# Turning x and B of the state-space mixer on VectorE and through DRAM instead of on TensorE, in token blocks two to four

## The chip, the cores and the metric

The kernel runs on one core of a Trainium2 chip. The metric is device time in microseconds (us), the median over executions; the kernel before has 2672.59 us (three runs, 2672.24 to 2672.9). Engines: TensorE (PE, its weight loads are PEld), VectorE (DVE), ScalarE (ACT), GpSimd (POOL); SyncE (SP) issues nearly all DMAs.

## The reference, cut to what matters

One hybrid decoder layer on 2048 tokens plus 16 meta tokens, float32, model width 1024. The mixer has a pooling part and a state-space part (SSD) with 4 groups of 6 heads of 64 channels, state size 128, chunks of 128 tokens. Then come an output projection, a feed-forward layer of 4096 and a norm.

```python
hn = rms_norm(h, norm_mix_w)
u, z, xbc, dt_raw = split(hn @ w_in)           # 512 | 1536 | 1536+512+512 | 24
xbc = silu(causal_dwconv(xbc))                 # x, B, C
# per group and chunk of 128 tokens; a_cs = cumsum(dt * a)
y_diag = ((C B^T) * decay) @ (x * dt)          # decay = exp(a_cs[l] - a_cs[s]), causal
state  = B^T @ (x * dt * decay_to_end)         # carried: S = S * chunk_decay + state
y_off  = (C @ S) * exp(a_cs)
y = (y_diag + y_off + d_skip * x) * silu(z)    # then a norm over the group's 384 channels
h = h + concat(pool(u), y) @ w_out
h = h + relu(rms_norm(h) @ w1)**2 @ w2
```

The convolution wants channels on the partitions and tokens along the row; `y_diag` and `state` want x and B with tokens on the partitions. Between the two stands a transpose of x (384 channels a group) and B (128 channels), and that is what is changed.

## The kernel before, in words

**Blocks and units.** The tokens go through the mixer in four blocks of 512 (`b` = 0 to 3; the prose counts them one to four), each with four chunks of 128 (`c`). The input projection is cut into units of 128 output columns. A group `g` has eight: unit 0 is B, 1 is C, 2 to 4 are x, 5 to 7 are z. Every product is split into high and low parts and made of three matmuls (`up_unit`). In blocks two to four the z units are computed as four pieces, one a chunk (`z_unit`), so a group there has nine items: five convolution units and four z pieces.

**From a unit to its tile.** TensorE fills one of two PSUM banks; ACT empties it (`evac`: four instructions for a convolution unit, which first wait until the item two before is finished); VectorE applies three taps (`taps`, L2387); ACT takes a tanh; VectorE finishes the SiLU (`finish`: L2417 for a convolution unit, L2403 for a z piece) into a tile of `F` (`group_tile`). The tiles of groups g and g+1 alternate.

**Steps.** A step `q` is one chunk of one group, 16 a block. `mixer_plan` lays step (g-1, c) beside items 2c and 2c+1 of group g (c = 3 also takes item 8); steps 12 to 15 have pool units beside them. TensorE's order in a step: unit `n1`; transposes of y of step q-2 (L2011); `diagonal` of q-1 (L2023); `slot1`: four transposes of x and B (L1985) into bank 4 or 5, then C B^T (L1991); `state` of q-1 (L2040); the unit or units `n2`; `y_offset` (L2003). In steps 12 to 15 there is no `n1`. `state` waits for `yo_ready`, the instruction L2600 of VectorE, which has emptied bank 7.

**VectorE's order in a step:** `y_finish` of q-1 (L2463, L2465), `state_add` (L2473), the taps of `n1`, the mask (L2555), the decay product (L2572), the low part of B (L2577), x times dt (L2583) and x times its weight (L2587), the low parts of y and of that product (L2486, L2478), `finish` of the item before and of `n1`, then L2600, then the taps of `n2`. `Steps.link` makes an instruction wait for the one before it on its own engine.

**ACT's order:** `evac` of n1, a tanh, the high part of C (L1526), six instructions of the decay (L1533), the exponential (L1539), the copies of B and x out of PSUM (L1547, L1549), then squares, the norm of y (L1433), high parts (L1428), the evacuation of n2.

**SyncE's queue** issues in program order: the weights of unit n when unit n-4 is done (`load`, L788, two DMAs of 512 KB a unit, a ring of four), the running sums (L804), the next block's x, h. Nothing is computed ahead by a planner; the order is written out as above. Everything outside the blocks' mixer (output projection, feed-forward) is not touched by the change. Block one (`b` = 0) uses plain, unsplit matmuls for `y_offset` and `state` and has z transposes besides.

Of the kernel before, what the change touches and what calls it, by code (L numbers as in the profile page):

```python
# [167 lines left out]
def build(nc, x, meta, norm_mix_w, w_in, pool_w, pool_scale, conv_w, conv_b, dt_bias, a_log,  # L168
          d_skip, ssm_norm_w, w_out, norm_ffn_w, w_ff1, w_ff2, norm_f_w, out):
    ctx = ExitStack()  # L170
    with ctx:
# [37 lines left out]
        xb = sb("xb", [P, GW])  # L209
        xdt = sb("xdt", [P, GW])  # L210
        xw = sb("xw", [P, GW])
        zs = sb("zs", [P, GW])
# [12 lines left out]
        acsT = win_tmp[0:HEADS, 0:TB]  # L225
        sums = sb("sums", [P, CH, HEADS_PER_GROUP, P])
# [30 lines left out]
        b_plain = at("b_plain", [P, 2, P], h_at + 9216)  # L257
# [31 lines left out]
        hn_scr = nc.dram_tensor("hn_scr", [3, 2, P, 4, TB], F32).ap()  # L289
        sums_scr = nc.dram_tensor("sums_scr", [BLOCKS, GROUPS, CH, HEADS_PER_GROUP * P], F32).ap()  # L290
# [15 lines left out]
        def per_head(t, c, g, rows=P):  # L306

            o = c * HEADS + g * HEADS_PER_GROUP
            return t[0:rows, o:o + HEADS_PER_GROUP].unsqueeze(2).to_broadcast(
                [rows, HEADS_PER_GROUP, HEAD])  # L310

# [44 lines left out]
        xb_ps = sig("xb_ps", STEPS)  # L356
        zc_ps = sig("zc_ps", STEPS)
        z_late = sem("z_late")
        xb_ready = sig("xb_ready", STEPS)
# [40 lines left out]
        w2_loaded = [sem(f"w2_loaded{i}") for i in range(5)]  # L400
# [15 lines left out]
        p_ps, p_hi, p_lo = sem("p_ps"), sem("p_hi"), sem("p_lo")  # L416
# [31 lines left out]
        def dt_bank(b):  # L448
            return bank[2] if b else bank[3]

# [179 lines left out]

        def w2_source(q):
# [70 lines left out]
        with nc.Block() as block:  # L702

            @block.sync
            def _(sp):
# [44 lines left out]
                initial = [s for s in signals if s.start and s not in (state_ready, *sums_loaded)]  # L750
# [56 lines left out]

                def load_quarter(i):
# [14 lines left out]
                for b in range(BLOCKS):  # L823
                    N0 = b * UNITS
                    for n in range(RING, U_OUT):
                        load(N0 + n, in_unit(n))
                        if b == 0 and RING < n < RING + 3:
                            meta_pair(POOL_PAIR + n - RING - 1)
                        if n == (8 if b else 12):
# [16 lines left out]
                    for d in range(2):  # L846
                        for i, kp in enumerate(OUT_ORDER):
                            load(N0 + U_OUT + d * 8 + i,
                                 w_out[0, kp * 256:(kp + 1) * 256, d * 512:(d + 1) * 512
                                       ].rearrange("(k p) c -> p k c", p=P))  # L850
                            if b < LAST and (d, i) == (0, 3):
# [3 lines left out]
                            if (d, i) == (0, 4 if b else 6):  # L855
                                yoff_ps.wait(sp, b, STEPS)
                                state_ps.wait(sp, b, STEPS)
                                sp.dma_start(h[:, :, :], x_in[0, b * TB:(b + 1) * TB, :].rearrange(
# [184 lines left out]
            def _(pool):  # L1043
# [61 lines left out]
                for b in range(BLOCKS):  # L1105
# [4 lines left out]
                    for q, g, c, n1, n2 in mixer_plan(b):  # L1110
# [12 lines left out]
                        xb_ready.wait(pool, b, q + 1)  # L1123
                        gated.wait(pool, b, q)
                        steps.link(nc.gpsimd.tensor_tensor(by_head(ty[:, :]), by_head(xb[:, :]),
# [105 lines left out]
                def second_sum(c, name):  # L1231
# [7 lines left out]
                    for x in {"t1": ("11", "12"), "t2": ("22",), "t3": (), "t4": ("21",)}[name]:  # L1239
                        l = 4 * c + W2_QUARTERS.index(x)  # L1240
                        pool.wait_ge(w2_loaded[l % 5], 16 * (l // 5 + 1))
# [31 lines left out]
            def _(act):  # L1273
# [42 lines left out]

                def evac(b, v):
# [3 lines left out]
                    up_out.wait(act, b, v - 1)  # L1321
                    piece = piece_of(b, v)
# [1485 lines left out]
```

## Time and profile before

| | |
|---|---|
| median of the runs | 2672.59 us |
| profiled execution, first to last instruction (span) | 2674.7 us |
| TensorE busy | 2654.5 us, 99% of the span |
| VectorE / ACT / GpSimd busy | 1636.3 / 1281.4 / 1091.7 us |
| TensorE's granted clock, mean | 0.999 |
| DMA traffic | 531.14 MB, mean 199 GB/s |

The profile comes from one execution; of that one the page has the span, which stands 2.1 us above the median of the unprofiled runs. Busy time says how much an engine does, not whether it is waited for; for that one reads the idle time of TensorE and what ended it, and then the timeline of a step, engine by engine. In a timeline row the third column is the engine, "x3" a number of instructions merged, and brackets give the idle time before the row and what ended it.

### The profile page before, as it was taken

What the parts mean: (1) busy time and instruction counts of PE and PEld (TensorE: products, weight loads), DVE (VectorE), ACT (ScalarE), POOL (GpSimd) and SP (SyncE); (2) the same over time, 40 slices, a digit from 0 to 9 for tenths busy, and PEclk for the clock granted to TensorE, in tenths of its full rate; (3) what the DMA queues carried; (4) which work ended last, traced back from release to release, by engine and by line L of the source; (5) the groups of instructions that cost most, each with busy time, mean ns of one, the idle gap of its engine ahead of it and who ended that gap; (6) DMA issues with size and microseconds to landing.
All of it is one profiled execution on the core that took longest, in us unless ns stands there. A gap on an engine that the chain in (4) does not pass through costs nothing.

```text
span 2674.7 us, 37670 instructions
## 1 busy us (share of the span) xinstructions
PE 2654.5 (99%) x14058; PEld 2225.0 (83%) x14058; DVE 1636.3 (61%) x2204; ACT 1281.4 (48%) x2562; POOL 1091.7 (41%) x866
## 2 busy tenths in 40 slices
PE   8999999999999999999999999999999999999998
PEld 6788778888888888898888888888888888888887
DVE  6788714788136883367853576574445766666667
ACT  4577654666245672355734454555454322222223
POOL 2133440335003441023444688665554535353434
PEclk9999999999999999999999999999999999999999
DMA  9977676654646546555574555774445842423324
GB/s 327 299 255 244 237 247 223 251 181 172 220 174 245 194 160 236 190 215 181 188 267 142 200 197 203 259 259 154 152 151 207 309 145 96 164 103 126 118 95 157
DMA packets 224451, 531.14 MB, mean 199 GB/s; under 512 B 14074, under 2 KB 97022, under 8 KB 214798
## 3 DMA queue, kind: packets, MB, share of 16 engines
q1 hardware_dynamic: 224270, 528.74, 55.3%
q8 instruction: 112, 1.84, 0.3%
q14 instruction: 69, 0.57, 0.1%
HBM read 382.74 MB, written 145.95 MB: 198 GB/s over the span
## 4 chain that ended last, share of the span: by engine, by line
PE 95%; DMA 2%; SPq 1%; DVE 1%; issue 0%; POOL 0%; ACT 0%; POOLq 0%; ACTq 0%
PE bank L2257 23%; PE bank L2225 22%; PE bank L1832 21%; PE bank L1939 12%; PE bank L1919 7%; PE bank L2023 2%; PE bank L1985 1%; PE bank L2040 1%; PE bank L2003 1%; PE bank L2011 1%; DMA w_scr<-w_both 1%; DMA meta_w<-in_w_in 1%; PE bank L1991 1%; PE bank L1958 1%; DMA raw<-in_w_out 0%
## 5 line engine op out<-in xcount | busy, mean ns | idle before, releaser
L1832 PE MATMUL bank<-hnT_hi,w_ring 128*128 128x512 f32 x1152 | 369.4, 392 | 0.0
L2257 PE MATMUL bank<-w_first,T_hi 128*128 128x512 f32 x896 | 275.8, 389 | 0.0
L2387 DVE SCALAR_TENSOR_TENSOR acc<-pre,par,acc 128x512 f32<-128x512 f32 x240 | 211.6, 882 | 90.4 <-ACT pre L1345 84.6
L1832 PEld LDWEIGHTS bank<-hnT_hi,w_ring 128*128 128x128 f32 x1152 | 216.3, 188 | 44.5 <-ACT win_tmp L1474 0.5
L2742 DVE TENSOR_TENSOR acc_th<-bank,acc_th 128x512 f32<-128x512 f32 x224 | 150.0, 686 | 155.4 <-PE bank L2257 154.0
L2225 PE MATMUL bank<-T_hi,w_both 128*128 128x512 f32 x768 | 242.4, 389 | 0.5 <-DVE ff L2683 0.5
L1939 PE MATMUL bank<-w_ring,T_hi 128*128 128x512 f32 x768 | 239.0, 392 | 0.1
L1832 PE MATMUL bank<-hnT_lo,w_ring 128*128 128x512 f32 x576 | 224.5, 390 | 0.0
L2257 PEld LDWEIGHTS bank<-w_first,T_hi 128*128 128x128 f32 x896 | 168.2, 188 | 34.9
L1919 PE MATMUL bank<-w_ring,hnT_hi 128*128 128x384 f32 x768 | 196.0, 336 | 0.0
L1832 PE MATMUL bank<-hnT_hi,w_both 128*128 128x512 f32 x544 | 183.1, 408 | 2.3 <-ACT pre L1345 2.3
L2225 PE MATMUL bank<-b,w_both 128*128 128x512 f32 x768 | 179.5, 389 | 0.0
L2257 PE MATMUL bank<-T_hi 128*128 128x512 f32 x448 | 174.3, 389 | 0.0
L2257 PE MATMUL bank<-T_lo,T_hi 128*128 128x512 f32 x448 | 174.3, 389 | 0.0
L2257 PE MATMUL bank<-w_first,T_lo 128*128 128x512 f32 x448 | 174.3, 389 | 0.0
L2257 PE MATMUL bank<-T_hi,T_lo 128*128 128x512 f32 x448 | 174.3, 389 | 0.0
L2225 PEld LDWEIGHTS bank<-T_hi,w_both 128*128 128x128 f32 x768 | 144.1, 188 | 31.2 <-DVE ff L2683 1.3
L2225 PEld LDWEIGHTS bank<-b,w_both 128*128 128x128 f32 x768 | 144.0, 188 | 30.3 <-DVE ff L2675 0.5
L1939 PEld LDWEIGHTS bank<-w_ring,T_hi 128*128 128x128 f32 x768 | 142.5, 188 | 30.0 <-DVE y L2465 1.3
L1630 ACT ACTIVATE w_both<-w_sum 128x512 fp32r<-128x512 f32 x128 | 81.0, 633 | 172.5 <-PE bank L2225 138.9
L2225 PE MATMUL bank<-hnT_hi,w_both 128*128 128x512 f32 x512 | 163.1, 389 | 0.0
L1706 ACT ACTIVATE T_hi<-third 128x1024 fp32r<-128x1024 f32 x56 | 56.3, 1053 | 220.4 <-PE bank L2257 207.7
(315 smaller groups left out, 6315.2 us busy)
## 6 DMA issues: line engine op xcount, KB each, us to landing
w_ring<-w_scr SPq DMA_DIRECT2D x312, 512.0 KB, 4.3
T_scr<-stage SPq DMA_DIRECT2D x32, 1792.0 KB, 6.7
w_scr<-w_both SPq DMA_DIRECT2D x100, 512.0 KB, 4.3
pair_raw<-in_w_ff SPq DMA_DIRECT2D x36, 1024.0 KB, 5.6
third<-T_scr SPq DMA_DIRECT2D x28, 1024.0 KB, 4.9
pair_raw<-T_scr SPq DMA_DIRECT2D x28, 1024.0 KB, 4.9
sums<-sums_scr SPq DMA_DIRECT2D x64, 384.0 KB, 5.0
raw<-in_w_in SPq DMA_DIRECT2D x36, 512.0 KB, 6.4
```

The costliest lines, as they stand in the source:

```text
L1630: nc.scalar.activation(hi, left_source(g), ACT.Copy).then_inc(w1_hi, 1)
L1706: nc.scalar.activation(hi[:, k, :], t_raw[x % 2][:, k, :], ACT.Copy).then_inc(t_hi, 1)
L1832: mm = nc.tensor.matmul(bank[s][:, :], w[:, k, :], t[:, k, :], start=(k == 0 and j == 0), stop=(k == KT - 1 and j == 2))
L1919: mm = nc.tensor.matmul(bank[s][:, 0:GW].rearrange("p (u c) -> p u c", c=P), t[:, k, tok], w[:, k, :, :], start=(k == 0 and j == 0), stop= ...
L1939: mm = nc.tensor.matmul(bank[4 + t][:, :], a, w[:, kk, :], start=(u == 0 and kk == 0 and j == 0), stop=(u == 7 and kk == 1 and j == 2))
L1958: mm = nc.tensor.transpose(dst[:, t * P:(t + 1) * P], h[:, t, k * P:(k + 1) * P], ident[:, :])
L1985: mm = nc.tensor.transpose(bank[4 + q % 2][:, i * P:(i + 1) * P], group_tile(g, j)[:, cols], ident[:, :])
L2023: mm = nc.tensor.matmul(bank[6][rows, r * HEAD:(r + 1) * HEAD], E[:, r, rows], xdt[:, r * HEAD:(r + 1) * HEAD], start=True, stop=True, til ...
L2225: mm = nc.tensor.matmul(bank1(p, m), w[:, k, :], t[:, k, :], start=(m not in (2, 7, 3) and k == 0 and j == 0), stop=(m not in (1, 6, 5) an ...
L2257: mm = nc.tensor.matmul(bank[4 * half + t][:, :], a[:, k, tok], w[:, k, :], start=(SECOND[q % 7] not in GOES_ON and k == 0 and j == 0), st ...
L2387: ins = nc.vector.scalar_tensor_tensor(acc[:, s, 0:TB], pre[:, s, k:k + TB], w, acc[:, s, 0:TB], ALU.mult, ALU.add)
L2742: ins = nc.vector.tensor_tensor(dst, src, dst, ALU.add)
```

## The change

In block one, TensorE still transposes; ACT copies x and B in one instruction into a new tile `xt` with a place for each of the four chunks. In blocks two to four:

- VectorE's `finish` of B and of the three x units writes the SiLU in place (B into its tile, since C B^T still needs it there), then, behind a link, turns it with `nc.vector.transpose`. That turns each 32x32 block in itself and leaves the blocks where they were.
- ACT's queue stores the turned tile, 256 KB, to a DRAM scratch, behind the evacuation of the item two later.
- SyncE's queue loads a chunk with four DMAs, each to 32 partitions, 16 pieces of 32 floats (128 bytes) a partition, so that the blocks come to their places. It waits until the group's four tiles are stored and the same chunk of the group before is used up.
- The four transposes of a step go from TensorE, and ACT's copy of x out of PSUM; the copy of B stays, from `xt`. VectorE and GpSimd wait for the chunk's DMAs in place of `xb_ready`.
- Semaphores are shared anew, `zs` moves, and block one's load of h waits for the last gated y.

```diff
                 def load_tokens(b, g, c):
+                    xt_stored.wait(sp, b, 48 * (g + 1))
+                    b_stored.wait(sp, b, 16 * (g + 1))
+                    ... # waits for xw_ready, ty_ready of the chunk's last user
+                    blocks = xt_scr[b, g, :, :, c * P:(c + 1) * P].rearrange(
+                        "t (i a) (j f) -> j a (t i) f", a=32, f=32)
+                    for j in range(4):
+                        sp.dma_start(xt[32 * j:32 * j + 32, c, :].rearrange("p (k f) -> p k f", f=32),
+                                     blocks[j]).then_inc(xt_loaded[c].sem, 16)
...
+                        if b and g and j in (0, 3, 4, 5):
+                            load_tokens(b, g - 1, (0, 3, 4, 5).index(j))
...
+                            if b and d == 0 and i < 2:
+                                load_tokens(b, GROUPS - 1, 2 + i)
...
                 def evac(b, v):
...
+                    evacuate(b, v, s, ps)
+                    store_turned(b, v - 2)
...
-                        xb_ps.wait(act, b, q + 1)
-                        ty_ready.wait(act, b, q)
-                        xw_ready.wait(act, b, q)
...
-                        nc.scalar.activation(xb[:, :], bank[4 + q % 2][:, 0:GW], ACT.Copy
-                                             ).then_inc(xb_ready.sem, 1)
+                        if b:
+                            xt_loaded[c].wait(act, b, 64 * (g + 1))
+                            state_ps.wait(act, b, q - 1 if q else 0)
+                            nc.scalar.activation(b_both[q % 2][:, 0, :], xt[:, c, GW:GW + P],
+                                                 ACT.Copy).then_inc(b_hi_ready.sem, 1)
...
-                    xb_ready.wait(pe, b, q - 1 if q else 0)
-                    for i, j in enumerate((2, 3, 4, 0)):
-                        mm = nc.tensor.transpose(bank[4 + q % 2][:, i * P:(i + 1) * P],
-                                                 group_tile(g, j)[:, cols], ident[:, :])
-                    mm.then_inc(xb_ps.sem, 1)
+                    if b == 0:
+                        ... # the same five lines
...
+                        dst = group_tile(g, 0) if j == 0 else pre[:, s, 0:TB]
+                        steps.link(nc.vector.scalar_tensor_tensor(dst, pre[:, s, 0:TB], 1.0,
+                                                                  acc[:, s, 0:TB], ALU.add,
+                                                                  ALU.mult))
+                        if j == 0 and g:
+                            b_stored.wait(dve, b, 16 * g)
+                            sums_stored.wait(dve, b, 16 * GROUPS)
+                        nc.vector.transpose(turn_tile(g, j), dst).then_inc(up_out.sem, 1)
```

VectorE in the third step (c = 2) of a group in block three, before, from the decay product to L2600:

```order
L2572 TENSOR_TENSOR E<-E,bank 128x768
L2577 TENSOR_TENSOR b_both_60<-bank,b_both_60 128x128
L2583 TENSOR_TENSOR xdt<-xb,dtt 128x384
L2587 TENSOR_TENSOR xw<-xb,dte 128x384
L2486 TENSOR_TENSOR T_lo<-bank,T_hi 128x3x128
L2478 TENSOR_TENSOR xw_both<-xw,xw_both 128x384
L2417 SCALAR_TENSOR_TENSOR F<-pre,acc 128x512 x2
L2600 TENSOR_TENSOR yo<-bank,ea 128x384
```

And the same place with the change (its line numbers are those of the changed kernel):

```order
L2650 TENSOR_TENSOR E<-E,bank 128x768
L2656 TENSOR_TENSOR b_both_59<-xt,b_both_59 128x128
L2662 TENSOR_TENSOR xdt<-xt,dtt 128x384
L2666 TENSOR_TENSOR xw<-xt,dte 128x384
L2564 TENSOR_TENSOR T_lo<-bank,T_hi 128x3x128
L2556 TENSOR_TENSOR xw_both<-xw,xw_both 128x384
L2489 SCALAR_TENSOR_TENSOR pre<-pre,acc 128x512
L2495 STREAM_TRANSPOSE F<-pre 128x512
L2489 SCALAR_TENSOR_TENSOR pre<-pre,acc 128x512
L2495 STREAM_TRANSPOSE F<-pre 128x512
L2679 TENSOR_TENSOR yo<-bank,ea 128x384
```

Two items are finished in this step, both of x: two more instructions stand ahead of the one that empties bank 7. In the steps c = 0 and c = 1 one such instruction is added, in c = 3 none.

TensorE at the same place of a step, before:

```order
L2003 MATMUL bank<-s_both,c_both 128x384 x3
L2011 MATMUL bank<-ident,y 128x128 x3
L2023 MATMUL bank<-xdt,E 64x64 x12
L1985 MATMUL bank<-ident,F 128x128 x4
L1991 MATMUL bank<-F 128x128
L2040 MATMUL bank<-xw_both,b_both_60 128x384 x3
```

With the change:

```order
L2068 MATMUL bank<-s_both,c_both 128x384 x3
L2076 MATMUL bank<-ident,y 128x128 x3
L2088 MATMUL bank<-xdt,E 64x64 x12
L2056 MATMUL bank<-F 128x128
L2106 MATMUL bank<-xw_both,b_both_59 128x384 x3
```

The four transposes are gone; C B^T and `state` follow `diagonal` at once.

SyncE's queue in block three, from the weights of the first three pool units to the next block's x, before:

```order
L788 DMA w_ring<-w_scr 128x1024 x6
L804 DMA sums<-sums_scr 128x768
L788 DMA w_ring<-w_scr 128x1024 x8
L853 DMA F<-in_x 128x4x1024
```

With the change:

```order
L809 DMA w_ring<-w_scr 128x1024 x6
L842 DMA xt<-xt_scr 32x16x32 x4
L825 DMA sums<-sums_scr 128x768
L809 DMA w_ring<-w_scr 128x1024 x2
L842 DMA xt<-xt_scr 32x16x32 x4
L809 DMA w_ring<-w_scr 128x1024 x2
L842 DMA xt<-xt_scr 32x16x32 x4
L809 DMA w_ring<-w_scr 128x1024 x4
L895 DMA F<-in_x 128x4x1024
```

Chunks two, three and four of the last group each stand behind weights that came before them in the queue.

## Rows read from the trace of the kernel before

**Rows 1.** The page's busy times, and TensorE's granted clock in 40 slices.

```profile
PE 2654.5 (99%) x14058; PEld 2225.0 (83%) x14058; DVE 1636.3 (61%) x2204; ACT 1281.4 (48%) x2562; POOL 1091.7 (41%) x866
...
PEclk9999999999999999999999999999999999999999
```

**Rows 2.** TensorE's waits: who, for whom, us in total, times, longest.

```profile
PE bank L1811 <- DVE F L2280: 5.8, 1, 5.8
```

**Rows 3.** Costliest groups by form, TensorE: the transposes of x and B, all blocks.

```profile
L1985 PE MATMUL bank<-ident,F 128*128 128x128 f32 x256 | 41.7, 286 | 0.0
```

**Rows 4.** Timeline of TensorE at slot1 of a third step: start, us, engine.

```profile
951.28 0.66 PE L1985 MATMUL bank<-ident,F 128*128 128x128 f32 x4
951.77 0.39 PE L1991 MATMUL bank<-F 128*128 128x128 f32 x2
```

**Rows 5.** Busy time from diagonal to L2600, block three, one group.

```profile
923.40:962.40 39.00, 39.00 (x257) 34.33 (x258) 36.72 (x54) 26.63 (x73) 15.23 (x20) 1.00 0.55 200
```

**Rows 6.** Timeline of that stretch: VectorE's links and the end at state.

```profile
923.38 0.56 DVE L2463 TENSOR_TENSOR y<-bank,ty 128x384 f32<-128x384 f32 x1 [5.65 <-PE bank L2023]
937.39 0.56 DVE L2463 TENSOR_TENSOR y<-bank,ty 128x384 f32<-128x384 f32 x1 [0.66 <-PE bank L2023]
938.72 0.56 DVE L2473 TENSOR_TENSOR S<-bank,S 128x384 f32<-128x384 f32 x1 [0.19 <-PE bank L2040]
...
948.81 2.79 DVE L2387 SCALAR_TENSOR_TENSOR acc<-pre,par,acc 128x512 f32<-128x512 f32 x3 [0.43 <-ACT pre L1345]
960.70 1.28 DVE L2417 SCALAR_TENSOR_TENSOR F<-pre,acc 128x512 f32<-128x512 f32 x2
961.90 0.55 DVE L2600 TENSOR_TENSOR yo<-bank,ea 128x384 f32<-128x384 f32 x1
...
963.29 0.60 PE L2040 MATMUL bank<-xw_both,b_both 128*128 128x384 f32 x2
```

**Rows 7.** Timeline of VectorE ahead of the steps: three linked taps.

```profile
776.87 2.33 DVE L2387 SCALAR_TENSOR_TENSOR acc<-pre,par,acc 128x512 f32<-128x512 f32 x3 [3.41 <-ACT pre L1345]
```

**Rows 8.** Groups by form of VectorE in the stretch of rows 5 and 6.

```profile
L2387 DVE SCALAR_TENSOR_TENSOR acc<-pre,par,acc 128x512 f32<-128x512 f32 x15 | 14.4, 962 | 0.8 <-ACT pre L1345 0.4
L2417 DVE SCALAR_TENSOR_TENSOR F<-pre,acc 128x512 f32<-128x512 f32 x5 | 3.3, 685 | 0.0
L2577 DVE TENSOR_TENSOR b_both<-bank,b_both 128x128 fp32r<-128x128 f32 x3 | 0.9, 284 | 0.0
```

**Rows 9.** Timeline of steps 2 and 3, the first group of block three.

```profile
840.29 0.56 DVE L2473 TENSOR_TENSOR S<-bank,S 128x384 f32<-128x384 f32 x1 [0.19 <-PE bank L2040]
849.41 0.55 DVE L2600 TENSOR_TENSOR yo<-bank,ea 128x384 f32<-128x384 f32 x1
...
850.85 0.78 PE L2040 MATMUL bank<-xw_both,b_both 128*128 128x384 f32 x3
```

**Rows 10.** Timeline of steps 13 and 14 of block three.

```profile
985.36 0.26 ACT L1547 ACTIVATE b_both<-bank 128x128 fp32r<-128x128 f32 x1
985.51 0.48 ACT L1549 ACTIVATE xb<-bank 128x384 f32<-128x384 f32 x1
988.85 0.61 ACT L1433 ACTIVATE y<-y,small 128x384 f32<-128x384 f32 x1
989.74 0.49 PE L2011 MATMUL bank<-ident,y 128*128 128x128 f32 x3
```

**Rows 11.** Timeline of SyncE's queue behind the last z piece.

```profile
972.43 2.73 SPq L788 DMA_DIRECT2D w_ring<-w_scr  x6
```

**Rows 12.** Busy time and DMA share while those weights move.

```profile
975.00:981.00 6.00, 6.00 (x29) 5.04 (x28) 5.84 (x11) 4.81 (x13) 3.19 (x5) 1.00 1.02 406
```

**Rows 13.** DMA packets while 96-byte pieces move, then 512-byte ones.

```profile
DMA packets 813, 0.12 MB, mean 202 GB/s; under 512 B 759, under 2 KB 813, under 8 KB 813
...
DMA packets 563, 0.29 MB, mean 320 GB/s; under 512 B 7, under 2 KB 562, under 8 KB 563
```

**Rows 14.** DMA issues of the page: x count, KB each, us to landing.

```profile
h_scr<-h SPq DMA_DIRECT2D x16, 512.0 KB, 2.6
```

More of the change, by code:

```diff
@@ L399, in build @@
         split_loaded = [sem(f"split_loaded{i}") for i in range(3)]
-        w2_loaded = [sem(f"w2_loaded{i}") for i in range(5)]
+        w2_loaded = [xt_loaded[i].sem if i < CH else sem("w2_loaded4") for i in range(5)]
         w2_sum_ready, w2_hi, w2_lo = sem("w2_sum_ready"), sem("w2_hi"), sem("w2_lo")
@@ L749, in _ @@
                     meta_pair(j)
-                initial = [s for s in signals if s.start and s not in (state_ready, *sums_loaded)]
+                initial = [s for s in signals if s.start and s not in (state_ready, xb_ps, xb_ready, b_hi_ready,
+                                                             *sums_loaded)]
                 for j in range(4, POOL_PAIR):
@@ L1121, in _ @@
                             inverse_root(b, rsy[:, :], ssy[:, :], ssy_ready, q, rsy_ready, 1)
-                        xb_ready.wait(pool, b, q + 1)
+                        x_tokens(pool, b, q)
                         gated.wait(pool, b, q)
-                        steps.link(nc.gpsimd.tensor_tensor(by_head(ty[:, :]), by_head(xb[:, :]),
+                        steps.link(nc.gpsimd.tensor_tensor(by_head(ty[:, :]), by_head(xt[:, c, 0:GW]),
                                                            per_head(dsk, 0, g), ALU.mult))
@@ L1315, in _, with store_turned @@
                 steps = Steps(act, act_sem)
+                def store_turned(b, v):
+                    n = unit_of(b, v) if b and v >= 0 else None
+                    if n is None or n >= U_POOL or n % UNITS_G not in (0, 2, 3, 4):
+                        return
+                    g, j = divmod(n, UNITS_G)
+                    act.dma_start(xt_scr[b, g, j - 2 if j else 3], turn_tile(g, j)
+                                  ).then_inc(xt_stored.sem if j else b_stored.sem, 16)
                 def evac(b, v):
@@ L1512, in _ @@
                             acsT_ps.wait(act, b, 1)
+                            if b:
+                                b_stored.wait(act, b, 16)
                             nc.scalar.activation(acsT, bank[3][0:HEADS, :], ACT.Copy
@@ L2423, in finish @@
                     up_evac.wait(dve, b, v + 1)
+                    if b:
+                        b_stored.wait(dve, b, 16 * GROUPS)
                     E_ = TB + 16
```

79 lines of the change are left out of this document (59 added, 20 removed).

## The prediction, made before the changed kernel ran

> **What bounds the kernel now.** I read the page's busy times first: TensorE is busy 99% of the span at its upper clock level, 2.4 GHz, the others 61% or less [rows 1]. Then its waits: the longest, 5.8 us, lies ahead of the blocks, and none is in the steps of blocks two to four [rows 2]. So each us taken from TensorE's queue there is a us of the kernel, as long as nobody it waits for becomes late. Then the cost of what goes [rows 3, 4]. Last, because the change loads VectorE, how near VectorE is to being waited for. Over the whole span it has 39% to spare, but an average says nothing here: in the 39 us of the first three steps of a group it is busy 36.72 [rows 5], since five convolution units are finished there, and idle only 5.65 us in the fourth step, just ahead [rows 6]. This is the view on which I decide.
>
> **What goes from TensorE.** Four transposes stand between diagonal and C B^T; from the first of them to C B^T 951.77 - 951.28 = 0.49 us pass [rows 4]. Their group has 41.7 us for 256 [rows 3], but a busy time leaves out overlap, so I take the distance of starts. 192 go: 48 steps by 0.49 = 23.5 us. That is the most the change can give.
>
> **What comes to VectorE.** 48 transposes of 128x512, 16 a block, and a link ahead of each. The trace has no VectorE transpose. Nearest rows: three linked instructions of 512 elements take 2.33, 0.78 each [rows 7]; two finishes without a link take 1.28, with 0.69 for the second, so the distance of two starts is 0.59 [rows 6, 8]. A finish with link and a transpose then take 0.78 + 0.59 = 1.37 in place of 0.59: x = 0.78 us for each turned tile. Bounds: an instruction of 128 elements takes 0.28 [rows 8], its start distance some 0.1 less, and with the link (0.19) x = 0.37, were the transpose so short; with both linked instructions at the taps' mean of 0.96, which GpSimd's work beside them makes long, x = 0.96 + 0.96 - 0.59 = 1.33. I take 0.78: the same operand width on the same engine, beside finishes that no one lengthens (mean 685 ns).
>
> The Trainium skill (VectorE: DVE Perf Modes, Rules for kernel authors) speaks against the change: a 128x128 transpose belongs on TensorE if PSUM will do as its destination, and VectorE is fastest only for 32x32. Its table of the three transpose paths gives 311 ns for a 128-column VectorE transpose. The nearest row has 284 ns at that width [rows 8]; by the page x would be some 0.03 more, an estimate, and the sum below 0.9 us more.
>
> **A group of three steps, where the two meet.** Follow VectorE from 923.38 in block three [rows 6]. It finishes B in c = 0 (+x), but had 0.66 us idle before y at 937.39, waiting for TensorE, and 0.19 before S at 938.72: it takes both up. In c = 1 one tile of x is turned (+x); 0.43 idle at 948.81, waiting for ACT, whose evacuation hangs on the unturned C tile, is taken up too. In c = 2 two tiles of x are turned (+2x), back to back, right ahead of L2600. So L2600 ends later by 4x - (0.66 + 0.19 + 0.43) = 4x - 1.28 = 1.84 us: 964.29 in place of 962.45. TensorE needs that end for state, which began at 963.29, 0.84 later. It would now come to it 4 x 0.49 = 1.96 earlier, at 961.33, and stands idle from there to 964.29. Against before, the stretch is longer by 1.84 - 0.84 = 1.00: the whole 1.96 is lost and 1.00 with it. This holds for the second and third group of units of each of three blocks: 6 x 1.00 = 6.0 us.
>
> In the first group of a block VectorE still waits for TensorE at the start of step 2 [rows 9]; TensorE is up to 1.5 us ahead there, so VectorE comes out of that wait at best 0.19 earlier than before and then has the two turned tiles: 2x - 0.19 = 1.37 later, with 850.85 - 849.96 = 0.89 to spare: 0.48 longer, three times: 1.4 us. Each of the nine stalls ends with a semaphore's way, some 0.05: 0.5 us.
>
> **Steps 12 to 15.** No tile is turned there, so the 0.49 could come through. But TensorE's next link is close: the norm of y ends at 988.85 + 0.61 = 989.46 and the transposes of y start at 989.74 [rows 10]. The norm stands behind ACT's high part of the weighted x, and that behind VectorE, diagonal and the exponential, so it does not move when ACT's copy of x (0.48) goes. I take 0.28 a step, bounds 0 and 0.49: 12 x 0.28 = 3.4 us gained, at most 5.9.
>
> **Edits at nothing.** ACT: 48 copies of x of 0.48 go [rows 10], 48 issues of some 0.45 come (six issues of SyncE take 2.73 [rows 11]); in the dense third step the issue lies ahead of a tanh that waits for VectorE's taps anyway; uncovered it would be 0.45 each in 9 third steps, 4 us. The four turned tiles ahead of a block's first step: VectorE idles 3.41 us ahead of an item's taps there [rows 7]; uncovered 4x a block, 9 us. SyncE: 192 issues; four stand ahead of the sums of the running decay once a block, 1.8 us, with the z pieces as cover; uncovered 5 us in all. Weights of the ring are asked for three units ahead. Block one, its single copy by ACT and the moved waits: TensorE's queue there is unchanged.
>
> **The sum.** 6 x 1.00 + 1.4 + 0.5 - 3.4 = +4.5 us; in general 30x - 18.9. The profiled span of 2674.7 would become 2679.2. The median of the runs lies 2.1 below the span; the same difference put on it gives **2677.1**. x = 0.37 gives -7.8, x = 1.33 gives +21; x = 0.63 is the point where nothing changes.
>
> **The chunk loads, and a rival from them (B).** Only chunk 1 of the last group is near: its four DMAs stand behind six of weights, issued from 972.43 [rows 11], and 3.15 MB at 406 GB/s [rows 12] take 7.7 us; with one us for the first packet to come, an estimate, they end at 981.2. A chunk is 2048 pieces of 128 bytes over 16 engines. Where 96-byte pieces move, 813 packets pass in 0.6 us, 11.8 ns an engine's packet; where 512-byte ones do, 563 in 0.9 us, 25.6 ns [rows 13]. So the chunk takes 1.5 to 3.3 us; I take 1.7, as the size is near the smaller. A store of 512 KB, 1.3 us by the same rate, lands after 2.6 [rows 14], so 1.3 is added: 984.2. ACT wants it at 985.36 [rows 10], or 0.28 earlier. It comes 0.9 us before that: no cost. Rival B: pieces of a row 2 KB apart cost more than those of rows 13, the chunk comes late, and ACT, GpSimd and VectorE stand in step 13 of each block, TensorE behind them. It decides from (0.9 + 1.7) / 128 = 20 ns a piece; at 25.6 it adds 0.7 us a block, 2 in all, at 60 it adds 5.1, 15 in all: 2679 to 2692.
>
> The Trainium skill (DMA: Bandwidth & Descriptors, Specifications) gives 512 bytes as the smallest transfer for line rate and says that shorter ones are read, modified and written. The rate falls here too, to 202 GB/s against 406 [rows 12, 13], but the time of a piece does not rise, so by this rule B would want more than these rows show.
>
> **Rival C, slower.** The transpose costs clearly more than an instruction of its width, or GpSimd's beside it stretches it: x of 1.0 to 1.33, +11 to +21: 2684 to 2694. For it speak the taps, 962 ns in the mean where undisturbed ones take 0.78 [rows 7, 8]; against it, that GpSimd works only 15.23 of the 39 us [rows 5] and the finishes themselves have a mean of 685 ns. It decides above x = 0.80 against the 0.2%.
>
> **Rival D, faster.** VectorE's 1.84 us are won back: the first three steps hold taps at a mean of 962 ns where undisturbed ones take 0.78 [rows 7, 8], 15 of them, 2.7 us a group, and if the shift parts VectorE from GpSimd's instructions, or x is near its lower bound, TensorE's 0.49 come through. With 1.5 us won back in each of nine stretches: 4.5 - 13.5 = -9, 2664; with all cover, -20, 2653. Against it: the order of both engines is the same, so they meet in the same places.
>
> **How the numbers follow.** A measurement of this kernel can tell 0.2%, 5.3 us. The forecast, VectorE takes the gain back, has 0.57, with its own range 2672 to 2682 (x 0.6 to 0.95): 0.41 of it within 0.2%, 0.16 slower. B has 0.13 (0.02 within), C 0.15, D 0.15 (0.02 within, 0.13 faster). Faster 0.13, same 0.45, slower 0.42. The range for 8 of 10 leaves out the outer part of D and of C: 2668 to 2689.
>
> **What would show it.** TensorE's waits name VectorE's L2679 (yo) at state, nine stalls of about 3 us, one in each c = 3 step; the transpose's row has about 0.7 us; TensorE's busy time falls by 20 us or so while the span does not; steps 12 to 15 take 0.28 us less each; the loads of chunk 1 land ahead of ACT's copy of B. Wrong would be: no such stalls (D), a transpose row above 0.9 (C), waits that name the DMA of xt (B).

## The result, and the profile after

| | |
|---|---|
| the changed kernel, median of 4 runs | 2692.56 us (2690.55 to 2694.2) |
| the kernel before, on the same chip, 4 runs | 2672.74 us (2672.24 to 2675.85) |
| ratio | 1.0069, 95% interval 1.0055 to 1.0083 |
| predicted | 2677.1 us, range 2668 to 2689 |

The change costs 19.8 us. The side that the sum gave (+4.5), slower, came out, but not for its reason: by the sum's own terms, the steps of TensorE and VectorE's end at state, the kernel became some 17 us faster, and the loss comes from a place that the prediction put at nothing. The profiled execution has a span of 2688.8 us, 14.1 above that of before, and the numbers below belong to it. (A run's time is 1.7 us above its span. So the profiled execution of the kernel before, 2674.7, stands 3.7 above the median of its runs, and that of the changed kernel 2.0 below: the spans are 5.7 us closer than the medians.)

The page: span, busy times, and the granted clock in 40 slices, to be read against [rows 1].

```profile
span 2688.8 us, 37665 instructions
PE 2643.9 (98%) x13866; PEld 2210.7 (82%) x13866; DVE 1647.1 (61%) x2252; ACT 1262.7 (47%) x2498; POOL 1115.4 (41%) x866
PEclk9999999999999999999999999999999999999999
```

TensorE has 10.6 us less to do, and the span is longer all the same: 24.7 us more in which it is idle. Whom it waits for stands in its waits (in each row: us in total, how often, the longest; of before [rows 2]):

```profile
PE bank L1983 <- DMA w_ring<-w_scr: 20.4, 3, 7.0
...
PE bank L1896 <- DMA w_ring<-w_scr: 2.7, 3, 1.4
PE bank L2076 <- ACT y L1491: 1.9, 2, 1.0
```

The first row is new: one wait of about 7 us a block, for weights. L1983 is `z_unit`, the pieces of the z units. No row names L2679 (yo) at state, the wait on which the prediction's sum rested. In block three, TensorE's timeline shows the wait:

```profile
841.48 0.77 PE L2106 MATMUL bank<-xw_both,b_both 128*128 128x384 f32 x3
848.96 0.98 PE L1983 MATMUL bank<-w_ring,hnT_hi 128*128 128x384 f32 x2 [6.71 <-DMA w_ring<-w_scr]
```

And the stretches around it (busy time of each engine, granted clock, DMA share, GB/s):

```profile
core 0: us, PE busy (x) PEld busy (x) DVE busy (x) ACT busy (x) POOL busy (x), PEclk, DMA share, GB/s
842.00:849.00 7.00, 0.29 (x3) 0.07 (x1) 6.77 (x13) 5.89 (x17) 4.70 (x6) 0.71 1.01 388
849.00:856.00 7.00, 7.00 (x24) 7.00 (x25) 2.92 (x4) 0.00 (x0) 0.37 (x1) 0.56 0.34 135
```

Two things are to be seen. The DMA engines are full while TensorE stands. And the granted clock falls within the wait, and behind it TensorE works at its lower level, 1.2 GHz, for most of the next 7 us: the first z piece, up to `y_offset`, takes 7.1 us here (5.8 and 6.6 in blocks two and four), in the kernel before 4.2 (840.09 to 844.26). That makes 6.9 us more in the three blocks.

SyncE's queue in the same block shows what stands ahead of those weights (in its rows the second column is how long the issue took; L809 weights, L825 sums, L842 token chunks, L885 hT):

```profile
812.88 6.51 SPq L842 DMA_DIRECT2D xt<-xt_scr  x4
819.43 2.48 SPq L825 DMA_DIRECT2D sums<-sums_scr  x1
821.96 0.43 SPq L885 DMA_DIRECT2D hT_scr<-hT  x1
822.44 3.82 SPq L809 DMA_DIRECT2D w_ring<-w_scr  x2
826.44 4.94 SPq L842 DMA_DIRECT2D xt<-xt_scr  x4
831.42 2.94 SPq L809 DMA_DIRECT2D w_ring<-w_scr  x2
...
838.62 1.95 SPq L809 DMA_DIRECT2D w_ring<-w_scr  x4
```

Four DMAs of a chunk need 1.9 us to be issued elsewhere; here one set takes 6.51. The same stretch of the kernel before, its DMA share first (and that of the us around 838), then SyncE's rows, then the first z piece:

```profile
807.00:838.00 31.00, 31.00 (x168) 25.66 (x166) 21.74 (x34) 17.09 (x50) 10.69 (x12) 1.00 0.96 368
837.50:838.50 1.00, 1.00 (x20) 0.76 (x20) 0.83 (x2) 0.67 (x2) 0.00 (x0) 1.00 0.12 45
```

```profile
811.65 0.52 SPq L845 DMA_DIRECT2D hT_scr<-hT  x1
812.21 7.05 SPq L788 DMA_DIRECT2D w_ring<-w_scr  x4
...
824.10 8.45 SPq L788 DMA_DIRECT2D w_ring<-w_scr  x4
```

```profile
840.09 0.52 PE L1919 MATMUL bank<-w_ring,hnT_hi 128*128 128x384 f32 x2
```

Here was the row that the prediction lacked. With no token traffic at all, the DMA engines are 96% busy for 31 us at the start of a block's steps, with weights, sums and the 2 MB of hT. The last z weights are asked for at 824.10 there, at 838.62 with the change. The engines come to rest just ahead of 838 (share 0.12 from 837.5 to 838.5; then the next unit's weights follow), and TensorE wants the z weights at 840.09: some 2.1 us of reserve. Three token chunks and two stores of turned tiles were put into that.

### The profile page after: what moved, and what is told of

It reads as the page before. It is cut to its first block, busy times and chain, and to the rows that moved or that the text cites. A ratio compares the mean times of both kernels' runs of the same rounds, so it can differ in the third digit from the quotient of the medians.

```text
span 2688.8 us, 37665 instructions
## 1 busy us (share of the span) xinstructions
PE 2643.9 (98%) x13866; PEld 2210.7 (82%) x13866; DVE 1647.1 (61%) x2252; ACT 1262.7 (47%) x2498; POOL 1115.4 (41%) x866
## 4 chain that ended last, share of the span: by engine, by line
PE 91%; DMA 3%; SPq 3%; DVE 1%; ACT 1%; issue 1%; POOL 0%; POOLq 0%; ACTq 0%; DVEq 0%
PE bank L2323 23%; PE bank L2291 22%; PE bank L1896 19%; PE bank L2003 13%; PE bank L1983 8%; PE bank L2088 2%; DMA w_ring<-w_scr 1%; PE bank L2106 1%; PE bank L2076 1%; SPq L842 1%; DMA w_scr<-w_both 1%; PE bank L2068 1%; PE bank L2056 1%; SPq L809 1%; PE bank L2022 1%
## 5 line engine op out<-in xcount | busy, mean ns | idle before, releaser
L1896 PE MATMUL bank<-hnT_hi,w_ring 128*128 128x512 f32 x1152 | 369.8, 392 | 2.7 <-DMA w_ring<-w_scr 2.7
L1896 PEld LDWEIGHTS bank<-hnT_hi,w_ring 128*128 128x128 f32 x1152 | 216.2, 188 | 48.5 <-issue 3.6
L2453 DVE SCALAR_TENSOR_TENSOR acc<-pre,par,acc 128x512 f32<-128x512 f32 x240 | 201.1, 838 | 82.6 <-ACT pre L1403 76.8
L1896 PE MATMUL bank<-hnT_lo,w_ring 128*128 128x512 f32 x576 | 224.6, 390 | 0.0
L1983 PE MATMUL bank<-w_ring,hnT_hi 128*128 128x384 f32 x768 | 201.4, 343 | 20.4 <-DMA w_ring<-w_scr 20.4
L1896 PE MATMUL bank<-hnT_hi,w_both 128*128 128x512 f32 x544 | 181.8, 405 | 0.8 <-ACT pre L1403 0.8
L1240 POOL TENSOR_TENSOR w_both<-w_sum,w_both 128x512 fp32r<-128x512 f32 x64 | 86.1, 1345 | 182.6 <-ACT w_both L1694 182.2
```

What stands on the lines that cost most here:

```text
L1240: nc.gpsimd.tensor_tensor(lo, left_source(g), hi.bitcast(F32), ALU.subtract).then_inc(w1_lo_pool, 1)
L1896: mm = nc.tensor.matmul(bank[s][:, :], w[:, k, :], t[:, k, :], start=(k == 0 and j == 0), stop=(k == KT - 1 and j == 2))
L1983: mm = nc.tensor.matmul(bank[s][:, 0:GW].rearrange("p (u c) -> p u c", c=P), t[:, k, tok], w[:, k, :, :], start=(k == 0 and j == 0), stop= ...
L2453: ins = nc.vector.scalar_tensor_tensor(acc[:, s, 0:TB], pre[:, s, k:k + TB], w, acc[:, s, 0:TB], ALU.mult, ALU.add)
```

## Experiments

Theory 1 is bandwidth: the engines are full, and whatever is ahead of the z weights in SyncE's queue makes them late. Theory 2 is the queue: the 2048 small pieces of a chunk fill it and SyncE can't issue. Theory 3 is the prediction's: VectorE at state.

**The store of hT earlier (x1).** In the changed kernel:

```diff
-                        if n == 11 and b:
+                        if n == 7 and b:
                             hT_ready.wait(sp, b - 1, KT)
                             sp.dma_start(hT_scr[b - 1], hT[:, :, :]).then_inc(hT_stored.sem, 16)
```

> The changed kernel, with the 2 MB store of hT issued behind the weights of unit 7, in a stretch where the DMA engines are idle, in place of unit 11. Theory 1 (the DMA engines are full from the start of a block's steps, and the token traffic puts the z weights behind): the store's 5.1 us of DMA time leave that stretch, the stall at the first z piece falls from 7.0 to about 2 us in each block, TensorE's clock stays up, 2692.6 - 3 x (5.1 + 4.5) = about 2664. Theory 2 (SyncE's queue stands because the 128-byte pieces fill it): the store has few descriptors, its place does not matter, the stalls stay at 7 and the time at 2692. Theory 3 (VectorE's transposes make state late, as predicted): no change, 2692.

Measured: 2681.13 (the kernel before in the same runs 2674.45; ratio 1.0025, 1.0015 to 1.0035). Theories 2 and 3, which wanted 2692, are out as the sole cause: some 11 us came back. But theory 1 wanted 2664.

```profile
PE bank L1896 <- DMA w_ring<-w_scr: 9.5, 3, 3.9
PE bank L1983 <- DMA w_ring<-w_scr: 7.2, 3, 5.7
```

The z waits fell from 20.4 to 7.2 in the sum (not evenly: one is still 5.7), and a wait of about 3 us a block came for an earlier unit, L1896. Its cause shows in a later run (x5).

**Large pieces (x2).** The changed kernel, same bytes and four DMAs a chunk, but contiguous rows (x and B don't come to their places):

```diff
-                        sp.dma_start(xt[32 * j:32 * j + 32, c, :].rearrange("p (k f) -> p k f", f=32),
-                                     blocks[j]).then_inc(xt_loaded[c].sem, 16)
+                        sp.dma_start(xt[32 * j:32 * j + 32, c, :],
+                                     xt_scr[b, g, c, 32 * j:32 * j + 32, :]
+                                     ).then_inc(xt_loaded[c].sem, 16)
```

> The changed kernel, with every chunk load of tokens made of 2048-byte pieces (128 of them in place of 2048): same bytes and the same four DMAs, but the blocks do not come to their places, so x and B are not in order. Theory 1: a chunk takes 128 x 87 ns / 16 = 0.7 us of the engines in place of 2.05, three chunks 4.1 us less in the full stretch, the stall falls from 7.0 to about 3 us, 2692.6 - 3 x 4.1 = 2680, or 2667 if the clock stays up too. Theory 2: no issue stands any longer and the stall is gone wholly, 2658. Theory 3: 2692.

Measured: 2681.2 (ratio 1.0027, 1.0017 to 1.0037), and

```profile
PE bank L1982 <- DMA w_ring<-w_scr: 12.0, 3, 4.1
```

The stalls fall from 7 to 4.0 us, near theory 1's 3 (and the time is its 2680); by theory 2 they had to vanish. So the small pieces cost 3 us a block by the DMA time that they take, 11 us in all with the clock.

**Only traffic, in the kernel before (x6, x7).** Nothing of the change, but hT stored once or twice more, in pieces of 16 KB (the counts that its readers wait for grow with it):

```diff
                             sp.dma_start(hT_scr[b - 1], hT[:, :, :]).then_inc(hT_stored.sem, 16)
+                            for m in range(2):          # one: range(1)
+                                sp.dma_start(copy_scr[b - 1, m], hT[:, :, :]).then_inc(hT_stored.sem, 16)
```

> The kernel before (TensorE's transposes, no token traffic), with hT stored two more times behind its store at unit 11: 10.2 us more of DMA time in few large pieces. Theory 1: the z weights landed 2.3 us before they were wanted, so a stall of 10.2 - 2.3 = 7.9 us appears at the first z piece of every block, and if the clock's fall comes from the idle time, some 4.5 us more each: 2672.7 + 37 = 2710; without the clock 2697. Theory 2: few descriptors, no stall, 2673. Theory 3: 2673.

> The kernel before with hT stored one more time behind its store at unit 11: 5.1 us more of DMA time, no small pieces. Theory 1: 5.1 - 2.3 = 2.8 us of stall at the first z piece of each block; with the two extra stores the stalls were 7.9, 7.4 and 6.7 and the clock fell after each. If the clock stays up after the shorter ones: 2674 + 8 = 2682; if it falls as it did: 2691. Rival (the engines had more slack than 2.3): no stall, 2674.

Measured: two copies 2702.26 (ratio 1.0100, 1.0086 to 1.0114), one copy 2683.22 (1.0033, 1.0020 to 1.0046). Waits with two, and then with one:

```profile
PE bank L1835 <- DMA w_ring<-w_scr: 22.0, 3, 7.9
```

```profile
PE bank L1835 <- DMA w_ring<-w_scr: 6.0, 3, 2.7
PE bank L1922 <- DMA w_ring<-w_scr: 1.5, 2, 1.1
```

The sizes are right (7.3 a block wanted at 7.9, 2.5 at 2.8), the place is not: most of the wait is one unit earlier (L1835, a convolution unit whose weights were asked for behind the copies), not at the z piece. Still, traffic alone, without a small piece and without VectorE's transposes, makes the kernel 28 us slower with two copies (10.2 us of DMA time a block, more than the change's) and 9 with one, for 22.0 and 7.5 us of waits. The rest of the 28 fits the clock: behind each of the three long waits TensorE works some 4 to 6 us at its lower level, behind one of those with a single copy only.

**SyncE's order rearranged (x5).** Store of hT behind unit 7, token chunks 2 and 3 of the first group behind units 15 and 16, chunk 1 of the last group earlier:

```diff
-                        if b and g and j in (0, 3, 4, 5):
-                            load_tokens(b, g - 1, (0, 3, 4, 5).index(j))
+                        late = {8: 0, 11: 1, 15: 2, 16: 3}
+                        if b and n in late:
+                            load_tokens(b, 0, late[n])
+                        spots = (0, 3, 4, 5) if g < GROUPS else (0, 1)
+                        if b and g > 1 and j in spots:
+                            load_tokens(b, g - 1, spots.index(j))
```

> The changed kernel, with three moves in SyncE's order: the store of hT behind unit 7, the token chunks 2 and 3 of a block's first group behind the weights of units 15 and 16 (before: 12 and 13), chunk 1 of the last group behind unit 33 (before: 35). Theory 1: 5.1 + 4.1 us leave the full stretch, the z weights are in time, no stall and no fall of the clock; 2692.6 - 3 x (7.1 + 4.5) - 2 x 1.3 = about 2655, faster than the kernel before. Theory 2: much the same, since the small pieces are moved behind the z weights. Theory 3: the stalls at state stay, 2690.

Measured: 2673.06 (ratio 0.9992, 0.9983 to 1.0001). The z waits and the wait in step 13 are gone, as theory 1 has it, 19.5 us are back. Not 37: TensorE's row, and below it one of SyncE's own waits in block three (785 to 812):

```profile
PE bank L1900 <- DMA w_ring<-w_scr: 10.1, 3, 4.0
```

```profile
SPq L842 <- DMA xt_scr<-F: 10.5, 1, 10.5
```

SyncE stood for 10.5 us at chunk 0, until the last turned tile had landed in DRAM, and behind it stood the sums and the weights of unit 9. It stood there in the changed kernel too, for 10.9 us; what is new is when that ends. Counted from the start of TensorE's z piece just ahead (790.88 in the changed kernel, 787.32 in x1, 784.98 in x5), chunk 0 is issued after 11.2, 14.6 and 15.0 us, and the weights of unit 9 after 17.9, 19.5 and 19.9. The store of hT, now just ahead, makes the tile stores land later: 2.6 us from issue in the median of 780 to 812 in the changed kernel, 5.4 and 5.8 in x1 and x5. So this is also the new wait of x1: a queue that waits in order passes a late store on to weights that have nothing to do with it.

**Chunk 0 behind unit 10 (y1, z1).** y1 has `late = {10: 0, 12: 1, 15: 2, 16: 3}` and hT behind unit 8; z1 the same with hT behind unit 7.

> The changed kernel with SyncE's order moved once more: hT stored behind unit 8, the four token chunks of a block's first group behind the weights of units 10, 12, 15 and 16, those of the last group's chunk 1 behind unit 33. In the run with the store behind unit 7 and chunk 0 behind unit 8, SyncE stood until the turned tiles and the sums had landed, so the weights of unit 9 were asked for 2.6 us after they could be. Theory 1: with the chunk behind unit 10 these waits (10.1 us) and the half level of the clock (8.5 us) go: 2673.1 - 18.6 = about 2654.5. Rival (the traffic is simply too much for these stretches, each move only moves the stall): waits of about 3 us a block again, 2670.

> The changed kernel with both moves: the store of hT behind unit 7 (the DMA engines are idle there) and chunk 0 behind unit 10, so that SyncE neither stands at the turned tiles nor puts 2 MB ahead of the weights of unit 9; chunks 1 to 3 behind 12, 15 and 16. The run with the store behind unit 8 still had 9.1 us of waits for weights in six places. Theory 1: each of these waits goes, 2670.6 - 9 = about 2661 in the median, 2658 in the profiled execution. Rival (too much traffic, a stall moves on): 2670 again.

Measured: y1 2670.62 (ratio 0.9990, 0.9981 to 0.9999), z1 2670.17 against 2674.47 for the kernel before in the same runs (ratio 0.9982, 0.9973 to 0.9992). By the medians both are faster than the kernel before, by some 4 us, with intervals that only just leave out no change; the times lie 16 and 9 us above the forecasts. In y1 and then z1 stand:

```profile
PE bank L1900 <- DMA w_ring<-w_scr: 4.8, 3, 1.7
PE bank L1987 <- DMA w_ring<-w_scr: 4.3, 3, 1.8
```

```profile
PE bank L1987 <- DMA w_ring<-w_scr: 6.7, 3, 2.9
```

In z1 the wait for unit 9 is gone, but at z, where x5 had none, there are three (1.5, 2.2, 2.9): chunk 0 now lies in the full stretch. The rival of these two expectations, a stall that moves on, was partly right.

**Two of the sums later (z2).** z1, and:

```diff
-                        if b and 9 <= n < 12:
-                            load_sums(b, 0, n - 8)
+                        if b and n in (9, 15, 16):
+                            load_sums(b, 0, {9: 1, 15: 2, 16: 3}[n])
```

> The same as the run with hT behind unit 7 and chunk 0 behind unit 10, and two of the four loads of running sums of a block's first group (384 KB each, chunks 2 and 3) behind the weights of units 15 and 16 in place of 10 and 11. Theory 1: some 2 us less DMA time ahead of the z weights in a full stretch; of the 6.7 us of waits at the first z piece (1.5, 2.2, 2.9) about 1.5 stay: 2670.2 - 5 = 2665 in the median, against 2674.5 before. Rival (the landing of the z weights hangs on when they are asked for, not on what is ahead of them): no change, 2670.

Measured: 2695.26 (ratio 1.0082, 1.0068 to 1.0095), a clear miss. No wait for z weights at the start of a block is left, as theory 1 said, but in its place stand these, one of ACT's in a stretch of block three (840 to 870) and one of TensorE's in the whole span (eight more, 10.0 us, for POOL's s_both):

```profile
ACT E L1597 <- DMA sums<-sums_scr: 7.8, 2, 6.6
```

```profile
PE bank L1900 <- ACT acc L1392: 12.1, 3, 4.2
```

The exponential waits for the sums, and everything hangs on that. I had counted what lies ahead of the weights and not the date at which the moved loads are themselves wanted.

**The move by itself (x8).** The kernel before with hT stored behind unit 7 (the edit of x1).

> The kernel before with only the store of hT moved, behind unit 7 in place of unit 11. Theory 1: its z weights came 2.3 us ahead of need anyway, nothing waits there, no change, 2673 to 2675. If instead the move is good by itself (less contention), it would be 5 or more faster, and part of the gain of the moved versions would not be the change's.

Measured: 2673.79, ratio 0.9998 (0.9989 to 1.0007): no change, as expected. The gain of y1 and z1 is not that of the moved store.

**Prices of the transposes (y2, y3, y4),** all made from y1, so that the stalls for weights are small. y2 leaves VectorE's transposes out and stores the unturned tiles; y3 has TensorE transpose in each step again, for nobody; y4 turns each tile twice.

```diff
 y2
-                        steps.link(nc.vector.scalar_tensor_tensor(dst, pre[:, s, 0:TB], 1.0,
 ...
-                        nc.vector.transpose(turn_tile(g, j), dst).then_inc(up_out.sem, 1)
+                        nc.vector.scalar_tensor_tensor(group_tile(g, j), pre[:, s, 0:TB], 1.0,
+                                                       acc[:, s, 0:TB], ALU.add, ALU.mult
+                                                       ).then_inc(up_out.sem, 1)
 y3
                     if b == 0:
                         xb_ready.wait(pe, b, q - 1 if q else 0)
-                        for i, j in enumerate((2, 3, 4, 0)):
 ...
+                    for i, j in enumerate((2, 3, 4, 0)):
+                        mm = nc.tensor.transpose(bank[4 + q % 2][:, i * P:(i + 1) * P],
+                                                 group_tile(g, j if b == 0 else 0)[:, cols],
+                                                 ident[:, :])
 ...
 y4
+                        steps.link(nc.vector.transpose(turn_tile(g, j), dst))
                         nc.vector.transpose(turn_tile(g, j), dst).then_inc(up_out.sem, 1)
```

> The same as the run with the moved order, but VectorE finishes x and B in one instruction into their tiles as before the change, and the unturned tiles are stored and loaded, so x and B are not in order. It prices VectorE's share. The prediction's sum (30x - 18.9 at x = 0.78) gives 18 to 23 us faster than with the transposes. By the trace of the changed kernel, where steps 6 and 10 take 11.00 us against 10.97 elsewhere and VectorE's end lies 0.05 before TensorE's wish, it is worth 0.1 us a step, under 2 us in all.

> The same as the run with the moved order, but TensorE makes four transposes in each step of blocks two to four again, with nobody using them. It prices TensorE's share. If the 0.49 us a step come through: 48 x 0.49 = 23.5 us slower. By the steps of the changed kernel (0.38 us shorter in the first three groups, 0.1 to 0.33 in steps 12 to 15): 15 to 18 us slower. If VectorE had taken the gain back: 0 to 3 slower.

> The same as the run with the moved order, but VectorE turns every tile twice, the second time with a link ahead: 0.71 + 0.19 = 0.9 us more for each tile. If VectorE is now at the edge ahead of state (its end 0.05 us before TensorE's wish in the third step of a group), four tiles make the first three steps 3.6 us longer in each group, nine times: about 32 us slower, or some 20 if only six stretches hang on it. If VectorE still has room: under 5 us slower.

Measured: y2 2671.58 (ratio 0.9990, the same as y1), y3 2684.7 (1.0039), y4 2696.89 (1.0089), against y1's 2670.62.

- y2: VectorE's 48 transposes cost this kernel nothing that can be told from zero (expected: under 2 us).
- y3: TensorE's cost 14.1 us by the medians; the spans are 13.1 apart (2666.8 and 2679.9), and y3 has 3.2 us less of waits for weights (5.9 against 9.1): 16.3 us, or 0.34 a step (expected: 15 to 18). That is the gain of the change on TensorE.
- y4: 26.3 us for a second transpose, between the two forecasts of 32 and 20. There the predicted stalls at state appear, nine of them:

```profile
PE bank L2110 <- DVE yo L2684: 11.3, 9, 1.3
```

So there is no room left on VectorE: turned once, it is just in time, and most of what comes on top is paid.

## Why the prediction was wrong

**The failed step** is the line under "Edits at nothing": "Weights of the ring are asked for three units ahead." In the program they are. But the transfer engines were full from there on and SyncE's queue stood: the last z weights were asked for at 838.62, 3.6 us before TensorE wanted them (842.25), and the time of asking is not the time of landing either (848.96). The share was looked up for the last group of a block alone [rows 12], where it falls, and taken there to judge chunk 1; the first group has the same loads plus all the sums and the store of hT. From the row above (96% busy to 838, z weights wanted at 840.09) it could have been worked out: reserve 2.1 us; three chunks at the prediction's own 1.7 us and two stores of 256 KB at 406 GB/s, 0.65 us each, are 6.4 us more, and TensorE comes some 0.8 earlier: a stall of 5.1 us, measured 6.7 to 7.0 (a chunk took 2.0 us there, not 1.7). Three times 5.1 on top of the prediction's 2677.1 makes 2692.4; that this is just the measured time is chance, since the errors below cancel. The term that carried the sum, VectorE's late end at state (+7.9 in nine stretches), failed as well, the other way; it is taken up below.

**The clock** was in no term. The three waits at L1983 are followed by TensorE's lower level, 6.9 us in all.

**Where the 14.1 us of span went:** 36 steps of 0.38, nine of 0.33 and three of 0.12 gained, -17.0; waits for weights 20.4 + 2.7; y in step 13 1.9; clock 6.9; and 3.0 us that are not the change's. In the profiled execution of the kernel before, TensorE stands 2.34 us ahead of the unit at 79.69 and then takes 7.1 us for it, since the granted clock falls:

```profile
80.00:85.00 5.00, 5.00 (x17) 3.98 (x15) 4.31 (x6) 3.81 (x8) 0.00 (x0) 0.66 1.04 341
```

The changed kernel's stands 0.76 us and takes 5.6, and its first diagonal starts at 109.21 against 112.16. All this adds up to 11.9; 2.2 us stay unexplained. TensorE's busy time fell by 17.0 in y1 too (2637.5 against 2654.5), but 1.6 of that is this unit at the lower level; what is left, 15.4, and the 16.3 of y3 say how well the 17.0 of the steps is known.

**TensorE's gain** was taken as 0.49 a step, 23.5 us, from the distance of starts [rows 4]. The steps became shorter by 0.38: diagonals of block three at

```profile
904.82 0.86 PE L2088 MATMUL bank<-xdt,E 128*64 128x64 f32 x22
915.82 0.92 PE L2088 MATMUL bank<-xdt,E 128*64 128x64 f32 x24
```

stand 11.00 us apart (before: 894.17 and 905.55, 11.38); the steps on both sides have 13.60 and 16.54 against 13.97 and 16.86. Over all steps 17.0 came in place of 23.5. Why the 0.49 between two starts is not 0.49 of the queue, no run here shows.

**VectorE at state.** The transpose's price was right: an undisturbed finish and transpose take 1.32 us (899.06 to 900.38, z1), where a finish alone was put at 0.59, so x is 0.73 against 0.78. (The 311 ns that the prediction takes from the Trainium skill (VectorE: DVE Perf Modes, The three transpose paths) is given there for bfloat16; this kernel turns float32, and no run here turns 128 columns on VectorE.)

```profile
899.06 0.65 DVE L2493 SCALAR_TENSOR_TENSOR pre<-pre,acc 128x512 f32<-128x512 f32 x1
899.75 0.71 DVE L2499 STREAM_TRANSPOSE F<-pre 128x512 f32<-128x512 f32 x1
900.38 0.52 DVE L2683 TENSOR_TENSOR yo<-bank,ea 128x384 f32<-128x384 f32 x1
```

What failed is that everything else on VectorE was held fixed. Its chain from y to yo over three steps took 39.07 us [rows 6] and should have taken 1.84 more; with the change it takes 38.28:

```profile
933.33 0.56 DVE L2541 TENSOR_TENSOR y<-bank,ty 128x384 f32<-128x384 f32 x1 [5.71 <-PE bank L2088]
971.09 0.52 DVE L2679 TENSOR_TENSOR yo<-bank,ea 128x384 f32<-128x384 f32 x1
```

2.6 us less than forecast. Where they come from stands in the groups of the same two stretches, 923.38 to 962.45 before, then 933.33 to 971.61 after ([rows 8] has the taps and finishes of before, 962 and 685 ns):

```profile
L2583 DVE TENSOR_TENSOR xdt<-xb,dtt 128x384 f32<-128x384 f32 x3 | 3.1, 1025 | 0.0
L2587 DVE TENSOR_TENSOR xw<-xb,dte 128x384 f32<-128x384 f32 x3 | 2.9, 968 | 0.0
```

```profile
L2453 DVE SCALAR_TENSOR_TENSOR acc<-pre,par,acc 128x512 f32<-128x512 f32 x15 | 13.1, 874 | 0.4
L2662 DVE TENSOR_TENSOR xdt<-xt,dtt 128x384 f32<-128x384 f32 x3 | 2.3, 772 | 0.0
L2666 DVE TENSOR_TENSOR xw<-xt,dte 128x384 f32<-128x384 f32 x3 | 1.6, 549 | 0.0
```

The two products with x gain 2.0 us, the fifteen taps 1.3; the five finishes of B, C and x lose 1.2 (two of them take 1.32 us); four transposes at 0.73 in place of 0.78 give 0.2. That makes 2.3 of the 2.6. GpSimd's and VectorE's products with x in one step show how, before, and then after:

```profile
901.07 0.83 POOL L1125 TENSOR_TENSOR ty<-xb,dsk 128x384 f32<-128x384 f32 x1
901.39 0.93 DVE L2583 TENSOR_TENSOR xdt<-xb,dtt 128x384 f32<-128x384 f32 x1
...
902.24 1.18 DVE L2587 TENSOR_TENSOR xw<-xb,dte 128x384 f32<-128x384 f32 x1
```

```profile
910.95 0.55 DVE L2662 TENSOR_TENSOR xdt<-xt,dtt 128x384 f32<-128x384 f32 x1
911.42 1.25 POOL L1169 TENSOR_TENSOR ty<-xt,dsk 128x384 f32<-128x384 f32 x1
911.42 0.55 DVE L2666 TENSOR_TENSOR xw<-xt,dte 128x384 f32<-128x384 f32 x1
```

The two engines still work side by side, but now GpSimd's instruction is the long one. So L2679 ends 0.05 us ahead of TensorE's state in steps 6 and 10 of a block, and the same instruction 1.49 ahead in y2. That is no reserve: the step that ends there takes 16.54 to 16.57 us, in y2 16.47, so a few hundredths are already paid. The predicted +1.00 in six stretches did not come; these stretches share the gain of 0.38 a step. That is what rival D described: it had 1.5 us won back in each stretch, 9 us faster than before, and 20 with all cover; 2.6 were won back, and the 17.0 of the steps lie between. D had a chance of 0.15 only, because the order of the engines is the same. Which of two engines side by side becomes longer hangs on more than the order. What decides it was not separated: in y3, where TensorE keeps the pace of before, x times its weight takes 763 ns in steps 4 to 6, against 970 before and 550 with the change in the same steps.

**Right:** the last four steps of a block (three of 0.33 and one of 0.12, in nine and three steps 3.3 us, 3.4 forecast; the weight load for y's transposes starts 0.05 us behind the end of the norm, having waited for it); the row of the transpose, 0.71 us; that VectorE has no room for more (y4); rival B's trigger, chunk 1 in step 13: the chunk was late in blocks two and four (ACT waits 1.5 and 1.2 us for it), 1.9 us of TensorE, where 0 was forecast and "2 in all" was B's lower end. B named the right resource and the wrong place; its rule "decides from 20 ns a piece" did not matter, since at the start of a block any transfer was too much.

## What to carry to other kernels

Before a change adds transfers, read the DMA share stage by stage, and for each load queued behind the new ones compare when the engines come to rest with when it is wanted: a mean of 199 GB/s hid a stretch of 31 us in which the engines were 96% busy. A moved load has two dates, what it delays and when it is wanted itself, and a queue that waits in order passes the wait for a store on to everything behind it. And a stall can cost more than its length: those of some 7 us here cost 1.6 to 2.9 us each on top, since TensorE came out of them at half speed.

## What the runs showed of the hardware

- An issue on SyncE's queue became longer when the DMA engines were full: 0.49 us for a DMA of 512 pieces of 128 bytes at 802.99, with the engines partly idle, 4.88 for the same DMA at 813.94 with them full. Weights of 4 KB pieces stand there too (4 issues in 7.05 us in the kernel before, waits included). The stalls of x2, x6 and x7 come out from DMA time alone, without a price for the long issues; but an issue holds up whatever SyncE has next.
- 2048 pieces of 128 bytes took 2.0 to 2.1 us of sixteen engines in the full stretch (6144 pieces, 16.0 ns each) and 1.6 ahead of it, with little beside them (2048 pieces from 803.07 to 805.38, 12.8 ns each).
- TensorE's granted clock: behind each wait for weights of 2.9 us or more (one in z1, three each in x1, x2, x5, x7 and the changed kernel) the trace shows the lower level, and then the upper one again; in y1, with waits of up to 1.8 us in the blocks, it does not. In between it went both ways: 1.00 in the 3.5 us behind a wait of 2.63 (x1, 813.50), but 0.68 in the 5.3 us behind one of 1.90 (y4, 465.70), and 0.66 behind the 2.34 us of the kernel before. So the length of a wait alone does not decide it. In the first of these windows it is z1, around its wait of 2.9 us, in the second x2, behind 4.0 us:

```profile
1181.00:1186.00 5.00, 4.85 (x19) 4.88 (x20) 4.77 (x10) 4.63 (x12) 3.57 (x5) 0.66 0.97 286
1186.00:1190.00 4.00, 4.00 (x25) 4.00 (x24) 3.93 (x6) 0.88 (x2) 1.05 (x1) 1.00 0.73 154
```

```profile
845.30:849.60 4.30, 4.29 (x16) 4.30 (x17) 4.15 (x8) 1.76 (x4) 2.51 (x3) 0.60 0.29 115
```

- A VectorE transpose of 128x512 float32 took 711 ns, little more than an elementwise instruction of that width without GpSimd beside it (685 ns).
